# Column sums made by adding transfers, issued at other times, and a layer's end by token tiles

## The reference

```python
for l in range(DEPTH):                       # the second model, DEPTH = 2
    mod = cond @ w_mod[l] + b_mod[l]
    h = rms_norm(x, norm_g[l, 0]) * (1.0 + sc1) + sh1
    y = mixer_block(h, ...)                  # four mixers, then w_o
    x = x + gt1 * rms_norm(y, norm_g[l, 1])
    h = rms_norm(x, norm_g[l, 2]) * (1.0 + sc2) + sh2
    y = jnp.square(jax.nn.relu(h @ w_up[l])) @ w_down[l]
    x = x + gt2 * rms_norm(y, norm_g[l, 3])
```

## Time and profile before

| | |
|---|---|
| three runs | 1927.97, 1931.34 (median), 1936.04 us |
| profiled execution | 1931.46 us, its span 1929.6 us |
| busy | PE 1833.3 us (95%), DVE 1365.6 (71%), ACT 927.1 (48%), POOL 131.4 (7%) |
| POOL's queue (q0) | 22912 packets, 67.11 MB, 15.7% of 16 engines' span |
| SP's queue (q1) | 59116 packets, 253.53 MB, 36.0% |

### The profile page before, as it was taken

How to read it: one execution, slowest core, us unless ns; L and a number is a source line. 1 busy time by engine, 2 the same in 40 slices (tenths; PEclk the granted TensorE clock), 3 DMA queues, 4 the chain that set the end, 5 groups by cost and what they waited for, 6 DMA issues and landing times.

```text
span 1929.6 us, 25385 instructions
## 1 busy us (share of the span) xinstructions
PE 1833.3 (95%) x9594; PEld 1443.4 (75%) x9594; DVE 1365.6 (71%) x2256; ACT 927.1 (48%) x1581; POOL 131.4 (7%) x122
## 2 busy tenths in 40 slices
PE   6999998999899888999988999999999999999997
PEld 3877566887566666776987888886777798888886
DVE  5897678886698687666666566777575577675767
ACT  4554443343323334446645446465345766464454
POOL 0003100000302122000000000300000000000020
PEclk9999999999999999999999999999999999999999
DMA  9566035885746978129999253342311223342533
GB/s 369 202 217 239 0 130 204 313 328 207 219 146 130 241 238 235 67 69 279 225 268 253 88 191 131 134 153 88 131 66 45 69 85 96 145 155 102 180 106 134
DMA packets 82141, 322.16 MB, mean 167 GB/s; under 512 B 6921, under 2 KB 8970, under 8 KB 67820
## 3 DMA queue, kind: packets, MB, share of 16 engines
q1 hardware_dynamic: 59116, 253.53, 36.0%
q0 software_dynamic: 22912, 67.11, 15.7%
HBM read 318.39 MB, written 69.21 MB: 201 GB/s over the span
## 4 chain that ended last, share of the span: by engine, by line
PE 72%; DVE 14%; DMA 6%; ACT 4%; issue 3%; SPq 0%; DVEq 0%; POOL 0%; ACTq 0%
PE banks L2569 9%; PE banks L2570 9%; PE banks L2571 9%; PE banks L3210 5%; PE banks L3211 4%; PE banks L3212 4%; PE banks L2939 3%; PE banks L2941 3%; PE banks L2940 3%; DMA w_raw<-in_wt 3%; PE banks L2833 2%; DVE mod_raw L1606 2%; PE banks L2754 2%; DMA down_raw<-col_sums 2%; PE banks L2853 1%
## 5 line engine op out<-in xcount | busy, mean ns | idle before, releaser
L2569 PE MATMUL banks<-h_high,w_high 128*128 128x512 f32 x888 | 351.0, 395 | 18.3 <-DVE w_low L1591 14.6
L2571 PE MATMUL banks<-h_high,w_low 128*128 128x512 f32 x888 | 347.1, 391 | 0.0
L2570 PE MATMUL banks<-h_low,w_high 128*128 128x512 f32 x888 | 347.1, 391 | 0.0
L2569 PEld LDWEIGHTS banks<-h_high,w_high 128*128 128x128 f32 x888 | 167.7, 189 | 61.3 <-DVE w_low L1591 20.1
L2570 PEld LDWEIGHTS banks<-h_low,w_high 128*128 128x128 f32 x888 | 167.8, 189 | 34.9 <-issue 0.7
L2571 PEld LDWEIGHTS banks<-h_high,w_low 128*128 128x128 f32 x888 | 167.5, 189 | 35.3
L1606 DVE CUSTOM_DVE_ANT_0 mod_raw<-mod_raw,cond_row 128x1024 f32<-128x1024 f32 x112 | 131.6, 1220 | 2.3 <-DMA mod_raw<-in_wmod 2.2
L2939 PE MATMUL banks<-h_high,w_high 128*128 128x512 f32 x288 | 115.2, 400 | 2.8 <-DVE w_low L2058 1.6
L1591 DVE TENSOR_TENSOR w_low<-w_raw,w_high 128x1024 fp32r<-128x1024 f32 x66 | 80.6, 1221 | 45.3 <-ACT w_high L639 45.0
L2941 PE MATMUL banks<-h_high,w_low 128*128 128x512 f32 x288 | 112.3, 390 | 0.0
L2940 PE MATMUL banks<-h_low,w_high 128*128 128x512 f32 x288 | 112.2, 390 | 0.0
(11 more groups left out here) (594 smaller groups left out, 4449.5 us busy)
## 6 DMA issues: line engine op xcount, KB each, us to landing
w_raw<-in_wt SPq DMA_DIRECT2D x96, 1024.0 KB, 5.8
mod_raw<-in_wmod SPq DMA_DIRECT2D x128, 512.0 KB, 5.6
col_sums<-in_wd POOLq DMA_DIRECT2D x4, 6144.0 KB, 28.7
col_sums<-in_wd POOLq DMA_DIRECT2D x12, 2048.0 KB, 32.0
down_raw<-col_sums SPq DMA_DIRECT2D x32, 768.0 KB, 8.5
col_sums<-col_sums POOLq DMA_DIRECT2D x8, 2048.0 KB, 29.7
down_raw<-in_wd SPq DMA_DIRECT2D x32, 512.0 KB, 4.2
mod_first<-in_wmod SPq DMA_DIRECT2D x8, 1024.0 KB, 10.6
```

The source lines that it names most:

```text
L2569: mm(out, high[:, k, :], H[:, k, :], start=k == order[0], stop=False)
L2570: mm(out, high[:, k, :], L[:, k, :], start=False, stop=False)
L2571: last = mm(out, low[:, k, :], H[:, k, :], start=False, stop=k == order[-1])
```

## The change

It moves the steps of the column sums and leaves what each does as it is. Layer 0's step 0 goes to the attention layer (first half, behind `pool_d`) and the first round of the long convolution (second half); its step 1 to the first and third round; its steps 2 and 3 into layer 0's mixers (behind `k_zero` and behind `gla_zero.1`). Layer 1's step 0 is issued in layer 0's mixers (behind the memsets of `GQ`, and behind `gla_zero.1`), its steps 1, 2 and 3 in layer 1's mixers. At a layer's end, token tile 2 is scaled on DVE and tile 3 on ACT; tiles 2 and 3 are turned into banks of their own and added to `X` one tile at a time (16 sums of 128 columns in place of 8 of 256).

```diff
+        column_sums(0, 0, 0)
+
         def out_accumulate(tag, last):
...
-            if n in (0, 1):
-                column_sums(0, n, 0)
-            if n == 3:
+            if n == 0:
                 column_sums(0, 0, 1)
+                column_sums(0, 1, 0)
+            if n == 2:
+                column_sums(0, 1, 1)
         for k in range(2):
...
-        column_sums(0, 1, 1)
         for m in range(2):
             pool.wait_ge(*when(f"fn_ps.{m}"))
...
-        for g in range(2):
-            column_sums(0, g, 2)
         out_accumulate("nf_h", 6)
-        for g in range(2):
-            column_sums(0, g, 3)
         for lay in led.each("layers", LAYERS):
...
             gp.memset(KC[:, :], 0.0).then_inc(*did("k_zero.all"))
+            for g in range(2):
+                if lay == 0:
+                    column_sums(0, g, 2)
+                else:
+                    column_sums(1, g, 1, "@0")
             pool.wait_ge(*when("v_tok.all"))
...
                 gp.memset(GQ[hp][:, :, :, :], 0.0).then_inc(*did("gla_zero.0" if hp else "gla_clear.0"))
+            if lay == 0:
+                column_sums(1, 0, 0)
+            else:
+                for g in range(2):
+                    column_sums(1, g, 2)
             pool.wait_ge(*when("gla_m.3"))
             pool.sem_inc(passed, 1)
             gp.memset(GA[:, :, :], 0.0).then_inc(*did("gla_zero.1"))
+            for g in range(2):
+                if lay == 0:
+                    column_sums(0, g, 3)
+                else:
+                    column_sums(1, g, 3)
             if lay == 0:
-                for g in range(2):
-                    for step in range(4):
-                        column_sums(1, g, step)
+                column_sums(1, 1, 0)
...
             token_root(2)
-            scaled(2)
             token_root(3)
+            scaled(3)
...
+            def token_sum(m, k):
+                turned = bank(TURNED[m - 1][k // 4])[:, k % 4 * P:k % 4 * P + P]
+                x = X[:, k * S + m * P:k * S + m * P + P]
+                v.scalar_tensor_tensor(x, turned, AF2[:, 24 + k:25 + k], x, mul, add).then_inc(*did(f"y2_x.{k}" if m == 3 else f"y2_xb.{k}"))
...
-            for k in range(4):
+            for k in range(2):
                 feature_sum(0, k)
-            dve.wait_ge(*when("y2_rs.3"))
-            rows = YT[:, 3, :, :].rearrange("p h c -> p (h c)")
-            v.tensor_scalar(rows, rows, STAT[:, 7:8], None, mul).then_inc(*did("y2_n.3"))
-            for k in range(4, KT):
+            dve.wait_ge(*when("y2_rs.2"))
+            rows = YT[:, 2, :, :].rearrange("p h c -> p (h c)")
+            v.tensor_scalar(rows, rows, STAT[:, 6:7], None, mul).then_inc(*did("y2_n.2"))
+            for k in range(2, KT):
                 feature_sum(0, k)
+            dve.wait_ge(*when("y2_mm.2"))
+            for k in range(KT):
+                token_sum(2, k)
             dve.wait_ge(*when("y2_mm.3"))
             for k in range(KT):
-                feature_sum(1, k)
+                token_sum(3, k)
```

More of the change, by code:

```diff
@@ L359, in program @@
     BANK_A, BANK_E, BANK_F, BANK_D = 4, 0, 2, 6
-    TURNED = ((0, 1, 6, 7), (2, 3, 0, 1))
+    TURNED = ((0, 1, 6, 7), (2, 3), (0, 1))
     HIDDEN_SQ2 = at(TAB_AT + 12 * KB, [P, 2 * S], name="hidden_sq")
@@ L612, in _ @@
                     raw, slot = BLOCKS[RAW_OF[w]], RAW_OF[w]
-                    own = "@0" if lay else ""
                     if w < PK:
                         sp.dma_start(raw[:, 0:2, :], whole[:, 0:2, :]).then_inc(*did(f"blocks{slot}.{c}.{w}.first", 16))
-                        sp.wait_ge(*when(f"colb{lay}{c // 2}.1{own}"))
+                        sp.wait_ge(*when(f"colb{lay}{c // 2}.1"))
                         sp.dma_start(raw[:, 2, :], summed[:, 3, :]).then_inc(*did(f"blocks{slot}.{c}.{w}", 16))
@@ L619, in _ @@
                         sp.dma_start(raw[:, 3, :], whole[:, 3, :]).then_inc(*did(f"blocks{slot}.{c}.{w}.first", 16))
-                        sp.wait_ge(*when(f"cola{lay}{c // 2}.3{own}"))
+                        sp.wait_ge(*when(f"cola{lay}{c // 2}.3"))
                         sp.dma_start(raw[:, 0:3, :], summed[:, 0:3, :]).then_inc(*did(f"blocks{slot}.{c}.{w}", 16))
@@ L1452, in _, with column_sums @@
         gp = nc.gpsimd
-        def column_sums(lay, g, step):
+        def column_sums(lay, g, step, made=""):
             n = PK * P * CHUNKS // 2
@@ L1458, in column_sums @@
             if step:
-                pool.wait_ge(*when(f"cola{lay}{g}.{step - 1}"))
+                pool.wait_ge(*when(f"cola{lay}{g}.{step - 1}{made}"))
             if step == 0:
@@ L1464, in column_sums @@
                 gp.dma_start(out[:, 2, :], whole[:, 3, :], accum_op=add).then_inc(*did(f"cola{lay}{g}.1", 16))
-                pool.wait_ge(*when(f"colb{lay}{g}.0"))
+                pool.wait_ge(*when(f"colb{lay}{g}.0{made}"))
                 gp.dma_start(out[:, 3, :], whole[:, 0, :], accum_op=add).then_inc(*did(f"colb{lay}{g}.1", 16))
@@ L2535, in feature_sum @@
                 turned = bank(TURNED[h][k // 2])[:, k % 2 * HS:k % 2 * HS + HS]
-                v.scalar_tensor_tensor(part(X, k, h), turned, AF2[:, 24 + k:25 + k], part(X, k, h), mul, add).then_inc(*did(f"y2_x.{k}" if h else f"y2_xa.{k}"))
+                v.scalar_tensor_tensor(part(X, k, h), turned, AF2[:, 24 + k:25 + k], part(X, k, h), mul, add).then_inc(*did(f"y2_xa.{k}"))
+            def token_sum(m, k):
+                turned = bank(TURNED[m - 1][k // 4])[:, k % 4 * P:k % 4 * P + P]
+                x = X[:, k * S + m * P:k * S + m * P + P]
+                v.scalar_tensor_tensor(x, turned, AF2[:, 24 + k:25 + k], x, mul, add).then_inc(*did(f"y2_x.{k}" if m == 3 else f"y2_xb.{k}"))
             seventh_sum(CHUNKS - 1, 1)
             dve.wait_ge(*when("y2_mm.1"))
-            for k in range(4):
+            for k in range(2):
                 feature_sum(0, k)
-            dve.wait_ge(*when("y2_rs.3"))
-            rows = YT[:, 3, :, :].rearrange("p h c -> p (h c)")
-            v.tensor_scalar(rows, rows, STAT[:, 7:8], None, mul).then_inc(*did("y2_n.3"))
-            for k in range(4, KT):
+            dve.wait_ge(*when("y2_rs.2"))
+            rows = YT[:, 2, :, :].rearrange("p h c -> p (h c)")
+            v.tensor_scalar(rows, rows, STAT[:, 6:7], None, mul).then_inc(*did("y2_n.2"))
+            for k in range(2, KT):
                 feature_sum(0, k)
+            dve.wait_ge(*when("y2_mm.2"))
+            for k in range(KT):
+                token_sum(2, k)
             dve.wait_ge(*when("y2_mm.3"))
             for k in range(KT):
-                feature_sum(1, k)
+                token_sum(3, k)
             if lay + 1 < LAYERS:
@@ L3258, in _ @@
                 for k in range(KT):
-                    if m == 2 and k == KT // 2:
+                    if m == 3 and k == 0:
                         pe.wait_ge(*when("y2_xa.3"))
-                    out = bank(TURNED[m // 2][k // 2])[:, k % 2 * HS + m % 2 * P:k % 2 * HS + m % 2 * P + P]
+                    if m < 2:
+                        out = bank(TURNED[0][k // 2])[:, k % 2 * HS + m * P:k % 2 * HS + m * P + P]
+                    else:
+                        out = bank(TURNED[m - 1][k // 4])[:, k % 4 * P:k % 4 * P + P]
                     last = nc.tensor.transpose(out, YT[:, m, :, :].rearrange("p h c -> p (h c)")[:, k * P:(k + 1) * P], IDENT)
```

## The result

The changed kernel takes 1910.84 us (median; 1909.78 to 1912.16), the kernel before 1932.69 in the same comparison (1927.97 to 1936.04): a ratio of 0.9889, 95% interval 0.9874 to 0.9903. It is faster by some 22 us. The forecast was 1905, with a range of 1897 to 1919: the sign and the range held, and the centre was 6 us too low.

The account below looks back on a forecast made before the run. The bound was taken as PE's own work plus places where PE stands still, some behind transfers beside adds. Gains of 5.8, 8.0, 5.8 and 12.7 against 5.8 lost gave -26.5, from 1931.46 to 1905 us; range 1897 to 1919.

Parts of the forecast that it names:

- Fourier: Fourier stage: table loads no longer stand behind step 1, so PE's 3.93 gap and 1.9 of half clock go: gain 5.8.
- Projection: Output projection, 656 to 713: step 2 leaves; of 11.4 us idle and clock loss, 3.4 stays for the ends: gain 8.0.
- Start of layer 0: Norm's root to third tile's copy: step 3 leaves, so layer 0's 31.69 becomes layer 1's 25.89: gain 5.8.
- Layer 0's down part: 930 to 1232: layer 1's steps leave, so 302.0 becomes the 289.3 layer 1 takes for the same products: gain 12.7.
- POOL's and SP's queues, the copies' new places: Attention layer, long convolution and queue waits: the moved transfers delay nothing there: 0, at most 1 in the long convolution.
- Layer 1's mixers: First weight pair, without slack, lands beside four adds 4.0 later, plus 1.8 of half clock: 5.8 lost.
- The second load: Layer 1's mixers, next weight pair: 0.9 late on ACT, hidden by PE's gap ahead of it: 0, at most 0.9.
- The layer's end: Both layers' ends: DVE's idle 1.57 goes, narrow sums at 0.3 each add 1.6: 0, between -1 and +1.
- A: Rival: the next wait takes over, freed stages give only lower bounds and layer 1 pays 7.9: 1917, chance 0.13.
- C: Rival: the change only swaps places, long convolution or layer 0's mixers wait as much as is freed: 1931, chance 0.07.
- B: Rival: slower, the mixers' loads have no cover and fourteen weight pairs each reach PE 4.0 later: 1955, chance 0.03.

Follow-up runs that it names:

- the kernel with one add: Changed kernel, but only the first of layer 1's four step-1 adds precedes the mixers' first weight pair, the others wait for the second pair's landing: 1911.86 us.
- the kernel that holds for two pairs: Changed kernel, but in layer 1 POOL issues the step-1 adds only after the mixers' first and second weight pairs have landed: 1900.55 us.
- the kernel with four adds earlier: Changed kernel, but layer 1's four step-1 adds are issued one load earlier, once the pair before the mixers' first has landed: 1907.18 us.

## Why the prediction was right, and where it missed

**Fourier (-5.8).** Right: -5.9, and putting the four adds back brings the gap and 5.0 us of it. The terms, the gap of 3.93 and the clock of 0.94, were both real: at that product PE has no gap any more, and the clock is 1.00.

**Projection (-8.0).** The mechanism was right, the size 2.2 short, and over the upper bound of 9.9 by 0.3. The step that failed is "of the 11.4 I leave 3.4 for the stage's ends". PE's idle time is now 46.80 - 44.64 = 2.16, not 3.4, and the clock is 1.00. That is 1.2 of the 2.2. The rest is in PE's busy time, which fell by 47.27 - 44.64 = 2.6 where the clock's term was 1.7; what the other 0.9 is stays open. What is late next is DVE, as the text had it: 45.54 of 46.80 us.

**Start of layer 0 (-5.8).** Right: 25.94 from root to third tile, where 25 to 26 was to show it; by PE's products -5.2.

**Layer 0's down part (-12.7).** Right to 0.1 us. To price a stage by the same code elsewhere in the same trace, without the disturbance, was the best-founded step of the sum.

**POOL's and SP's queues, the copies' new places (0).** Right. Nothing between 198 and 270 got longer, and no PE gap from there to 612 grew by more than 0.4 us.

**Layer 1's mixers (+5.8).** The place and the mechanism were right: the load without slack, the gap ahead of it, the half clock behind it. Its size was wrong, 10.0. The step that failed is "the nearest are three pairs beside adds in 906 to 932 us, 8.2 to 9.9 with a median of 8.7". They are near in time, but not in what decides: each was issued 6.5 us or more behind the last transfer that POOL had issued. This one follows the first add by 1.6. The load came 12.33 - 4.74 = 7.6 later, not 4.0, and the gap grew by 7.6. The clock took (1 - 0.50) x 5.2 = 2.6, not 1.8: together 10.2. The bounds did hold it (0 to 11.4). The trace of before had the right row, and it wasn't read: a weight pair issued by SP 1.95 us behind a copy of POOL's. POOL's timeline, SP's, and the landing of that pair:

```profile
862.59 0.81 POOL L1461 DMA_DIRECT2D col_sums<-in_wd  x1
863.38 0.78 POOL L1462 DMA_DIRECT2D col_sums<-in_wd  x1
...
864.54 0.33 SPq L487 DMA_DIRECT2D w_raw<-in_wt  x1
...
DMA to landing us min/median/max: 12.3/12.3/12.3
```

With 7.6 later in place of 4.0 the sum would have been 3.6 higher, 1908.6. Nobody waited for that pair, so it had left no gap; only its landing time shows it.

**The second load (0).** Right, and by more than was claimed: with a hold for the first pair the second came in 11.4, ACT waited 3.2, and PE saw nothing.

**The layer's end (0).** The 0 came out, but not as it was worked out. Both terms were real: 1.57 of idle time gone, 1.0 of narrow sums added (0.26 each, forecast 0.3). So they don't cancel, and DVE ends 0.7 us earlier. Between the layers this comes through (PE's gap ahead of the last turning is 0.56 in place of 1.29); behind the last layer the stores, which the sum didn't name, take it back and 0.3 more. That so little is left is luck.

**The rivals.** A (1917) and C (1931) didn't come: each freed stage gave what was forecast to within 0.6 us, or more. A's other half did come, as layer 1 paid 10.0 where A had 7.9. B (1955) named the right mechanism, and its condition was met by one load only. The next five pairs in layer 1, from 1345.78 to 1399.83, landed in 8.1 to 9.5 us and nobody waited for them. Two more pairs, issued 1.95 us behind the first of POOL's transfers at 842.52 and 1452.79, took 11.85 and 11.88, and nobody waited for these either.

## What to carry to other kernels

When a background transfer is moved, list the foreground loads that are issued behind each of its new issue times, those within some 5 us above all, and price each by a load of the old trace that stands equally far behind such an issue, not by one that is near on the clock. Then look which of those loads has no cover; a wait that issues the background transfer behind that load's landing was worth 10 us here, where issuing it one load earlier was worth 4 by the trace. Where the same code runs twice in a trace, once with and once without the disturbance, the difference is the forecast.

## What the runs showed of the hardware

Behind a transfer that POOL issues, a load of SP's is late in two parts. Alone, a 1 MB pair has its first packet 0.97 us after its issue and lands 3.8 us after that. In the kernel with one add, that pair has no packet for 5.45 us. The records of the DMA queues from its issue at 1332.85 to 1338.25, when its first packet comes, hold q0's packets alone, which are POOL's; q1 is SP's queue (columns: packets, MB, share of 16 engines):

```profile
q0 software_dynamic: 177, 0.36, 76.4%
```

and from then to its landing, both queues (q1 also carries a 1 MB load of compression weights issued right behind it):

```profile
q1 hardware_dynamic: 205, 1.55, 56.2%
q0 software_dynamic: 310, 0.63, 50.8%
```

In the kernel without column sums the same pair's packets begin 0.97 us after the issue. Its records from 1333.9 to 1337.9, over the landing:

```profile
q1 hardware_dynamic: 187, 1.40, 91.7%
```

Taken over the traces of this study with POOL's transfers in them, weight pairs with no other load of SP's under way show two bands. The 19 that were issued within 2 us of the first of POOL's transfers under way took 11.5 to 12.3 us, behind copies as behind adds, and five more with the compression weights' load right behind them 12.0 to 12.3; the 8 that were issued 4.9 us behind it took 8.9 to 9.8. Later ones are mostly at 8 to 10, at a few places up to 11.6, and down to 4.8 where POOL's transfers were about to end. In full flow of POOL's transfers the first packet mostly comes 3.5 us after the issue (3.48 for the pair issued at 1358.20 in the kernel that holds for two pairs, 3.45 for the first pair in the kernel with four adds earlier). At some places it comes as late as just behind an issue: the pair at 883.02 in the kernel before, 20 us behind the copies, had its first packet after 4.93 us and took 10.6. So the distance to the issue tells where the longest waits surely are, not where all of them are.

This bears on the rule of the Trainium skill named in the prediction ("DMA: Bandwidth & Descriptors", "Queues, rings and completion order": a DMA engine takes turns between queues packet by packet). The trace is in keeping with it once the load's packets flow: 3.8 us became 6.7. It doesn't account for the 5.45 us in which the load had no packet at all. The prediction's estimate from the rule, with turns of equal length, was at most twice 4.7; the measurement, 12.3, decides. What holds back the first packet no run here shows.

The other finding is the clock. Behind one and the same gap of PE, 0.73 us ahead of the turning of the softmax's probabilities in layer 0's mixers, half clock lasted 10.2 us in the changed kernel, 10.2 without any column sums, and 3.4 in the kernel that holds for two pairs, where the next 6.8 us ran at full clock. In the kernel with layer 1's steps back in layer 0 there was none behind it (1.00 from 884 to 892). The rows are of the tables of stages, in this order:

```profile
881.00:891.30 10.30, 10.03 (x127) 6.65 (x126) 7.88 (x14) 8.39 (x16) 0.00 (x0) 0.50 0.99 306
```

```profile
883.70:893.90 10.20, 9.91 (x126) 6.66 (x126) 7.78 (x14) 8.42 (x16) 0.00 (x0) 0.50 0.30 104
```

```profile
886.80:890.20 3.40, 3.40 (x22) 2.39 (x20) 3.29 (x6) 3.40 (x8) 0.00 (x0) 0.50 1.03 340
890.20:897.00 6.80, 6.80 (x110) 4.11 (x112) 5.74 (x8) 6.74 (x12) 0.00 (x0) 1.00 1.00 299
```

The DMA share is 0.30 in the one long stretch and 0.99 in the other, so the long one comes without adds too. By matched products the stretch up to 897 is 2.6 us shorter in the kernel that holds for two pairs than in the one without column sums, and layer 0's mixers as a whole 1.4 us, as the products behind it then wait. That is more than any of the small lines of the account that were put at 0. Why half clock lasts longer in one execution than in another no run here shows.
